# Final stage of a hybrid decoder step: sums of residual and expert rows moved from VectorE to TensorE for four of nine tiles

## The chip, the cores and the metric

The kernel runs on one core of one Trainium2 chip. The metric is the device time of one execution in microseconds (us), lower is better. Engine names in the views: PE is TensorE's matmul, PEld its weight load, DVE is VectorE, ACT is ScalarE, POOL is GpSimd, SP is SyncE; SPq and ACTq are the DMA issues of SP and ACT.

## The reference

One decoder layer over 1048 rows (16 meta tokens, 1024 prompt tokens, 8 sample tokens) of width 1024, fp32. After the mixers (short gated convolution and gated DeltaNet), each row goes through a hierarchical mixture of experts, which picks two of 32 experts per row, and a final RMSNorm:

```python
def _rmsnorm(x, w):
    x32 = x.astype(jnp.float32)
    y = x32 * lax.rsqrt(jnp.mean(x32 * x32, axis=-1, keepdims=True) + EPS) * w.astype(jnp.float32)
    return y.astype(x.dtype)
...
    x = x + jnp.concatenate([y_a, y_b], axis=-1) @ w_out
    x = x + _moe(_rmsnorm(x, norm_ffn), rg_w, rg_b, re_w, re_b, w_gate, w_up, w_down)
...
    y_prompt = _rmsnorm(xp, norm_final)[:, N_META:]
    y_sample = _rmsnorm(xs, norm_final)
```

For the final stage this means: each row of the result is the residual row x plus two expert rows, divided by the root of the mean of its squares, times the weight row `norm_final`.

## The kernel before

The kernel runs in stages: a front stage with the input projection and the mixers, a short stage for the sample tokens, a routing stage with the output projection and the router, the expert stage, and the final stage. The residual rows stay in SBUF as `b.x1`, [128, 9, 1024]. The expert stage takes one expert block of up to 128 rows after the other: GpSimd gathers its rows, TensorE transposes them (`turn`, L1811) and multiplies them (`gate_up`, L1829, and `down`, L1854), ACT and VectorE scale the halves of the product (L1865, L1872), and GpSimd scatters them to a DRAM tensor `b.ye` (L1802) that has two rows for each token, one per chosen expert. 32 blocks run in the main part, and up to 16 overflow blocks behind it, each in a branch (`further`, L1904); in this execution two of them are taken.

The final stage is `final_parts` (L2030). It works on nine tiles of 128 rows, the last of 24 rows. It has no program of its own on the engines: its parts are called at the end of each engine's program of the expert stage.

- SP (`loads`) first waits until all scatters have landed, a chain of branches over the overflow blocks (L1942). Then it issues, for each tile t, the loads of `y0[t]` (L2046) and `y1[t]` (L2047), 512 KB each, without a wait between them, and after tile 0 the load of the weight row `wn` (L2049). Each tile has its own buffers, in SBUF that the expert weights used before.
- VectorE (`scales`) waits for `wn`. For each tile it waits for both loads of the tile, adds `y0` to `x1` (L2086) and `y1` to `x1` (L2088), and then scales the tile before (L2080): row times rstd times `wn`, written over `y1`. So its order is add 0, add 1, scale 0, add 2, scale 1, and so on to add 8, scale 7, scale 8.
- ACT (`norms`) takes for each tile the sum of squares (L2062, with an accumulator read), Ln (L2065) and Exp (L2068), and then issues the store of the tile before (L2057), once it is scaled.
- TensorE has nothing to do in this stage.

Of the kernel before, what the change touches and what calls it, by code (L numbers as in the profile page):

```python
# [9 lines left out]
ALU = mybir.AluOpType  # L10
ACT = mybir.ActivationFunctionType
# [10 lines left out]
TILES = 9  # L22
# [59 lines left out]
def later(i):  # L82

    return not isinstance(i, int) or i > 0
# [1684 lines left out]
def expert_stage(nc, m, s, b, io):  # L1769

    ps = b.psum
# [10 lines left out]
    q = {n: s.pair("e_" + n) for n in names}  # L1782
# [23 lines left out]
    def turn(pe, q, k):  # L1806

        for g in range(2):
            for j in range(4):
                kk = 4 * g + j  # L1810
                ins = nc.tensor.transpose(ps[:, 2 + g, j * P:j * P + C], xg[k][:, kk:kk + KD * (P - 1) + 1:KD],  # L1811
                                          b.ident[0:C, 0:C])
        ins.then_inc(q.turned, 1)
# [9 lines left out]
    def gate_up(pe, q, p, n, k):  # L1823
        pe.wait_ge(q.xt_ok, 2 * n + 2)
        for g in range(2):
            for f in range(KF):
                o = (g * KF + f) * P
                for kk in range(KD):
                    ins = nc.tensor.matmul(ps[:, p, o:o + C], b.slots[k][g][:, kk, f * P:f * P + P],  # L1829
                                           xt[p][:, kk, :], start=(kk == 0), stop=(kk == KD - 1))  # L1830
        ins.then_inc(q.gu_ok, 1)
# [15 lines left out]
    def down(pe, q, p, n, k):  # L1847
        pe.wait_ge(q.he_ok, n + 1)
        if later(n):
            pe.wait_ge(q.outa_ok, n)  # L1850
            pe.wait_ge(q.outb_ok, n)
        for c in range(2):
            for f in range(KF):
                ins = nc.tensor.matmul(ps[0:C, 4 + 2 * p + c, :], he[p][:, f, :],  # L1854
                                       b.slots[k][2][:, f, c * 512:c * 512 + 512], start=(f == 0), stop=(f == KF - 1))
        ins.then_inc(q.down_ok, 1)
# [25 lines left out]
    def staggered(eng, front, mid, back):  # L1882

        front(block_of(0))
        front(block_of(1))
        mid(block_of(0))
        for j in range(4):
            front(block_of(j + 2))
            mid(block_of(j + 1))
            back(block_of(j))  # L1890
        with eng.Fori(1, 7) as i:
            for j in range(4):
                front(block_of(j + 2, i))
                mid(block_of(j + 1, i))
                back(block_of(j, i))
        for e in (30, 31):
            front(block_of(e))
            mid(block_of(e - 1))
            back(block_of(e - 2))
        mid(block_of(31))  # L1900
        back(block_of(30))
        back(block_of(31))

    def further(eng, body):  # L1904

        count = eng.to_reg(eng.value_load(b.ove[0:1, OV:OV + 1], min_val=0, max_val=OV))

        def both(n):
            for p in range(2):
                with eng.If_lt(eng.to_reg(2 * n + p), count):  # L1910
                    body(2 * n + p, p, n)

        both(0)
        with eng.Fori(1, OV // 2) as n:
            both(n)
        return count

    def nothing(x):
        pass

    final = final_parts(nc, m, s, b, io)

    with nc.Block() as block:
        @block.sync
        def _(sp):
            with sp.Fori(0, 7) as i:
                for k in range(4):
                    sp.wait_ge(main[k % 2].down_ok, 2 * i + k // 2 + 1)
                    load_expert(sp, b, io, 4 * i + 4 + k, k)

            def body(v, p, n):
                if later(n):
                    sp.wait_ge(more[p].down_ok, n)
                else:
                    sp.wait_ge(main[p].down_ok, NE // 2 - 1)
                e = sp.value_load(b.ove[0:1, bass.ds(v, 1)], min_val=0, max_val=NE - 1)
                load_expert(sp, b, io, e, p, more_w[p])
            count = further(sp, body)
            for p in range(2):
                sp.wait_ge(main[p].scattered, 16 * (NE // 2))  # L1940
            for v in range(OV):
                with sp.If_lt(sp.to_reg(v), count):  # L1942
                    sp.wait_ge(more[v % 2].scattered, 16 * (v // 2 + 1))
            final.loads(sp)
# [59 lines left out]
        @block.tensor  # L2004
        def _(pe):
            def front(x):
                if later(x.last_n):
                    pe.wait_ge(x.last.xt_ok, 2 * x.last_n)
                pe.wait_ge(gathered[x.k], 16 * (x.r + 1))
                turn(pe, x.q, x.k)  # L2010

            def mid(x):
                pe.wait_ge(b.w_landed[x.k], 48 * (x.r + 1))
                gate_up(pe, x.q, x.p, x.n, x.k)

            staggered(pe, front, mid, lambda x: down(pe, x.q, x.p, x.n, x.k))
            for p in range(2):
                pe.wait_ge(main[p].outa_ok, NE // 2)
                pe.wait_ge(main[p].outb_ok, NE // 2)

            def body(v, p, n):
                pe.wait_ge(more_gathered[p], 16 * (n + 1))
                turn(pe, more[p], p)
                pe.wait_ge(more_w[p], 48 * (n + 1))
                gate_up(pe, more[p], p, n, p)
                down(pe, more[p], p, n, p)
            further(pe, body)


def final_parts(nc, m, s, b, io):  # L2030

    m.at = b.R2
    y0 = [m.place(f"y0_{t}", [P, D]) for t in range(TILES)]
    y1 = [m.place(f"y1_{t}", [P, D]) for t in range(TILES)]
    wn = m.place("wn", [P, D])
    w_in, e_in, add0, x2_ok, sq, ln, rs, o_ok, left = (
        s("wn_in"), s.pair("ye_in", TILES), s("f_add"), s("x2_ok"), s("f_sq"), s("f_ln"), s("f_rs"), s("f_ok"),
        s("y_out"))

    def rows(t):  # L2040
        return P if t < 8 else LAST

    def loads(sp):
        for t in range(TILES):
            n = rows(t)
            sp.dma_start(y0[t][0:n, :], b.ye[t * P:t * P + n, :]).then_inc(e_in[t], 16)  # L2046
            sp.dma_start(y1[t][0:n, :], b.ye[TOK + t * P:TOK + t * P + n, :]).then_inc(e_in[t], 16)  # L2047
            if t == 0:
                sp.dma_start(wn[:, :], io.norm_final.partition_broadcast(P)).then_inc(w_in, 16)  # L2049

    def norms(act):
        nc.scalar.preload_act_table_set("natural_log_exp_and_others")

        def send(t):
            n = rows(t)
            act.wait_ge(o_ok, t + 1)
            act.dma_start(io.y[t * P:t * P + n, :], y1[t][0:n, :]).then_inc(left, 16)  # L2057

        for t in range(TILES):
            n = rows(t)  # L2060
            act.wait_ge(x2_ok, t + 1)
            nc.scalar.activation(y0[t][0:n, :], b.x1[0:n, t, :], ACT.Square, accum_out=b.stat[0:n, t, 0:1]  # L2062
                                 ).then_inc(sq, 1)
            act.wait_ge(sq, t + 1)
            nc.scalar.activation(b.stat[0:n, t, 1:2], b.stat[0:n, t, 0:1], ACT.Ln, scale=1.0 / D,  # L2065
                                 bias=b.eps[0:n, :]).then_inc(ln, 1)
            act.wait_ge(ln, t + 1)
            nc.scalar.activation(b.stat[0:n, t, 2:3], b.stat[0:n, t, 1:2], ACT.Exp, scale=-0.5).then_inc(rs, 1)  # L2068
            if t >= 1:
                send(t - 1)  # L2070
        send(TILES - 1)
        act.wait_ge(left, 16 * TILES)

    def scales(dve):
        dve.wait_ge(w_in, 16)

        def scale(t):
            n = rows(t)
            dve.wait_ge(rs, t + 1)
            nc.vector.scalar_tensor_tensor(y1[t][0:n, :], b.x1[0:n, t, :], b.stat[0:n, t, 2:3], wn[0:n, :],  # L2080
                                           ALU.mult, ALU.mult).then_inc(o_ok, 1)

        for t in range(TILES):
            n = rows(t)
            dve.wait_ge(e_in[t], 32)
            nc.vector.tensor_tensor(b.x1[0:n, t, :], b.x1[0:n, t, :], y0[t][0:n, :], ALU.add).then_inc(add0, 1)  # L2086
            dve.wait_ge(add0, t + 1)
            nc.vector.tensor_tensor(b.x1[0:n, t, :], b.x1[0:n, t, :], y1[t][0:n, :], ALU.add).then_inc(x2_ok, 1)  # L2088
            if t >= 1:
                scale(t - 1)  # L2090
        scale(TILES - 1)

    f = Shared()
    f.loads, f.norms, f.scales = loads, norms, scales
    return f


# [75 lines left out]
```

## Time and profile before

| | us |
|---|---|
| runs shown, median of 3 | 1212.77 |
| lowest and highest | 1210.85, 1213.52 |
| the profiled execution, its own time | 1210.12 |
| its span in the trace | 1208.3 |
| busy: PE / DVE / ACT / POOL | 1026.7 / 450.9 / 371.7 / 158.3 |

The span is the time from the first to the last record of the profiled execution. The granted clock is the share of TensorE's 2.4 GHz that it was given; 0.50 is 1.2 GHz. A DMA share of 1.00 means that the sixteen DMA engines of the core were busy all the time. The two levels to keep apart are the shares over the whole span and what happens in the last 43 us, where the final stage lies (its first load is issued at about 1165 us).

### The profile page before, as it was taken

The page shows a single profiled execution, that of the slowest core. Times are in us where ns is not written, and L with a number is a line of the kernel's source. Part 1 is how long each engine was busy: PE and PEld are TensorE (multiplying, and loading weights), DVE is VectorE, ACT ScalarE, POOL GpSimd, SP SyncE. Part 2 cuts the span into 40 slices and gives each one's busy share as a digit, 9 for nine tenths or more (in the row PEclk, how much of TensorE's full clock was granted, in tenths as well). Part 3 has the DMA queues.
Part 4 walks back from the last instruction along what each step waited for, and adds up shares of the span by engine and source line. Part 5 has one row for each costly group of instructions (what it writes and reads, how often), then busy time and mean ns, then how long its engine had stood idle before and what let it go on. Part 6 is the DMA issues. An engine that isn't in the chain of part 4 may idle for free. (4 is left out here: it accounts for less than half of the span.)

```text
span 1208.3 us, 16435 instructions
## 1 busy us (share of the span) xinstructions
PE 1026.7 (85%) x6572; PEld 917.4 (76%) x6572; DVE 450.9 (37%) x666; ACT 371.7 (31%) x736; POOL 158.3 (13%) x145
## 2 busy tenths in 40 slices
PE   5779999979999999584999914999999999999720
PEld 4669999979999999573777614888888888887510
DVE  5356777892534352334222163111111111111028
ACT  5466776323334343103222100122122121121114
POOL 3011111211101010020000012021121221211000
PEclk9899999999999999766999956999999999999875
DMA  5103666427555541373111174388878878888047
GB/s 205 28 32 109 154 152 165 126 71 225 148 140 146 151 136 24 119 283 122 70 70 70 39 300 175 121 321 316 334 300 307 328 293 321 320 334 314 33 150 298
DMA packets 117658, 221.97 MB, mean 184 GB/s; under 512 B 68316, under 2 KB 81686, under 8 KB 108766
## 3 DMA queue, kind: packets, MB, share of 16 engines
q1 hardware_dynamic: 106618, 199.66, 49.4%
q0 software_dynamic: 9792, 17.19, 3.8%
q10 hardware_dynamic: 1188, 4.29, 0.9%
q8 instruction: 41, 0.67, 0.2%
q14 instruction: 19, 0.16, 0.0%
HBM read 192.33 MB, written 47.26 MB: 198 GB/s over the span
## 5 line engine op out<-in xcount | busy, mean ns | idle before, releaser
L1085 PE MATMUL psum<-hh,wh 128*128 128x350 f32 x672 | 227.8, 339 | 13.1 <-ACT acc L649 8.1
L1085 PE MATMUL psum<-hh,wl 128*128 128x350 f32 x672 | 221.6, 330 | 0.0
L1085 PE MATMUL psum<-hl,wh 128*128 128x350 f32 x672 | 221.1, 329 | 0.0
L1085 PEld LDWEIGHTS psum<-hh,wh 128*128 128x128 f32 x672 | 131.0, 195 | 15.4 <-ACT acc L649 8.6
L1829 PE MATMUL psum<-xgt,wg 128*128 128x128 f32 x1088 | 131.6, 281 | 4.4 <-ACT xgt L1820 4.4
L1829 PEld LDWEIGHTS psum<-xgt,wg 128*128 128x128 f32 x1088 | 128.9, 198 | 5.4 <-issue 5.4
L1085 PEld LDWEIGHTS psum<-hl,wh 128*128 128x128 f32 x672 | 130.9, 195 | 0.9
L1085 PEld LDWEIGHTS psum<-hh,wl 128*128 128x128 f32 x672 | 130.4, 194 | 0.0
L1829 PE MATMUL psum<-xgt,wu 128*128 128x128 f32 x1088 | 127.1, 275 | 0.0
L1854 PE MATMUL psum<-wd,he 128*128 128x512 f32 x272 | 122.4, 593 | 2.8 <-DVE he L1844 2.8
L1829 PEld LDWEIGHTS psum<-xgt,wu 128*128 128x128 f32 x1088 | 124.2, 192 | 0.0
L569 POOL TENSOR_TENSOR wl<-wst,wh 128x1024 fp32r<-128x1024 f32 x28 | 67.9, 2426 | 395.5 <-ACT wh L592 395.5
L1841 DVE SCALAR_TENSOR_TENSOR ge<-thx,psum 128x256 f32<-128x256 f32 x34 | 14.3, 422 | 279.2 <-ACT thx L1835 279.2
L1854 PEld LDWEIGHTS psum<-wd,he 128*128 128x128 f32 x272 | 49.2, 191 | 52.4 <-issue 49.2
L848 DVE SCALAR_TENSOR_TENSOR acc<-raw,cqw,acc 128x1072 f32<-128x1072 f32 x36 | 70.3, 1953 | 26.9 <-ACT acc L631 26.0
L1835 ACT ACTIVATE thx<-psum 128x256 f32<-128x256 f32 x34 | 13.0, 383 | 212.1 <-PE psum L1829 212.1
L1802 POOL DMA_INDIRECT expert_rows<-out,slot_rows x34 | 34.1, 1004 | 335.1 <-DVE out L1872 275.2
L1716 PE MATMUL psum<-wo_hi,yt_hi 128*128 128x512 f32 (+1 forms) x144 | 47.9, 415 | 19.6 <-DVE wo_lo L1562 19.6
L1865 ACT ACTIVATE out<-psum,slot_w 128x512 f32<-128x512 f32 x34 | 23.4, 687 | 110.2 <-PE psum L1854 110.2
L1811 PEld LDWEIGHTS psum<-ident,xg 128*128 128x128 f32 x272 | 36.8, 192 | 25.4 <-issue 17.2
L1872 DVE TENSOR_SCALAR out<-psum,slot_w 128x512 f32<-128x512 f32 x34 | 25.5, 751 | 80.6 <-PE psum L1854 80.6
L1820 ACT ACTIVATE xgt<-psum 128x512 f32<-128x512 f32 x68 | 36.9, 595 | 51.8 <-PE psum L1811 45.8
(322 smaller groups left out, 1342.6 us busy)
## 6 DMA issues: line engine op xcount, KB each, us to landing
wg<-w_gate SPq DMA_DIRECT2D x34, 1024.0 KB, 4.9
wu<-w_up SPq DMA_DIRECT2D x34, 1024.0 KB, 8.0
wd<-w_down SPq DMA_DIRECT2D x34, 1024.0 KB, 11.8
wst<-w_in SPq DMA_DIRECT2D x28, 512.0 KB, 4.2
y<-expert_rows SPq DMA_DIRECT2D x16, 512.0 KB, 11.1
ck<-qkv_rows SPq DMA_DIRECT2D x9, 702.0 KB
qkv_rows<-acc SPq DMA_DIRECT2D x12, 520.0 KB, 6.1
xb<-x SPq DMA_DIRECT2D x8, 512.0 KB, 4.1
```

Source lines behind the costliest of these rows:

```text
L569: nc.gpsimd.tensor_tensor(wl[n % 3][:, :, :], wst[n % 3][:, :, :], wh[n % 2][:, :, :].bitcast(F32), ALU.subtract).then_inc(wl_ok, 1)
L848: stt(ac[:, 0:QLEN], rw[:, q:q + QLEN], w[:, q:q + 1], ac[:, 0:QLEN], ALU.mult, ALU.add).then_inc(taps if q < KQ - 1 else conv_ok, 1)
L1085: ins = mm(ps[:, c, 0:ZC], w[:, kk, :], a[:, kk, c * ZC:(c + 1) * ZC], start=(kk == 0 and q == 0), stop=(kk == KD - 1 and q == 2))
L1716: ins = mm(ps[0:n, 2 * (t % 2) + c, :], y, w[:, c * 512:c * 512 + 512], start=(kk == 0 and q == 0), stop=(kk == KD - 1 and q == 2))
L1802: pool.indirect_dma_start(b.ye, bass.IndirectOffsetOnAxis(ap=b.slot_rows[:, 1, e:e + 1].bitcast(U32), axis=0), out[p][:, :], None, bounds_ ...
L1811: ins = nc.tensor.transpose(ps[:, 2 + g, j * P:j * P + C], xg[k][:, kk:kk + KD * (P - 1) + 1:KD], b.ident[0:C, 0:C])
L1820: nc.scalar.activation(xt[p][:, 4 * g:4 * g + 4, :], bank4(ps, 2 + g, P, C), ACT.Copy).then_inc(q.xt_ok, 1)
L1829: ins = nc.tensor.matmul(ps[:, p, o:o + C], b.slots[k][g][:, kk, f * P:f * P + P], xt[p][:, kk, :], start=(kk == 0), stop=(kk == KD - 1))
L1841: nc.vector.scalar_tensor_tensor(ge[p][:, :, :], th[p][:, :, :], 1.0, g[:, 0:KF], ALU.add, ALU.mult).then_inc(q.ge_ok, 1)
L1854: ins = nc.tensor.matmul(ps[0:C, 4 + 2 * p + c, :], he[p][:, f, :], b.slots[k][2][:, f, c * 512:c * 512 + 512], start=(f == 0), stop=(f == ...
L1865: nc.scalar.activation(out[p][:, 0:512], ps[0:C, 4 + 2 * p, :], ACT.Copy, scale=weight(e)).then_inc(q.outa_ok, 1)
L1872: nc.vector.tensor_scalar(out[p][:, 512:D], ps[0:C, 5 + 2 * p, :], weight(e), None, ALU.mult).then_inc(q.outb_ok, 1)
```

## The change

For tiles 0, 2, 4 and 6 (`SUMMED`) TensorE makes the sum of `x1`, `y0` and `y1` in PSUM: each of the three is multiplied by the identity (`b.ident`) as the stationary operand, in two products of 512 columns, and the six products of a tile accumulate in two banks. The four tiles use two pairs of banks in turn, so tile 4 waits until tile 0 is scaled, and tile 6 until tile 2 is. The products of the residual rows of tiles 0 and 2 are issued before the wait for any load. ACT's square and VectorE's scaling of these tiles read PSUM. VectorE makes no additions for them. The other five tiles stay as they are. The order of the tiles on each engine is not changed.

```diff
             further(pe, body)
+            final.sums(pe)
...
+SUMMED = (0, 2, 4, 6)
...
+    def in_psum(t):
+        return ps[0:rows(t), 2 * bank_of(t):2 * bank_of(t) + 2, :]
...
         for t in range(TILES):
             n = rows(t)
-            act.wait_ge(x2_ok, t + 1)
-            nc.scalar.activation(y0[t][0:n, :], b.x1[0:n, t, :], ACT.Square, accum_out=b.stat[0:n, t, 0:1]
-                                 ).then_inc(sq, 1)
+            if t in SUMMED:
+                act.wait_ge(summed, SUMMED.index(t) + 1)
+                nc.scalar.activation(y0[t][0:n, :].rearrange("p (c n) -> p c n", c=2), in_psum(t), ACT.Square,
+                                     accum_out=b.stat[0:n, t, 0:1]).then_inc(sq, 1)
+            else:
+                act.wait_ge(x2_ok, added.index(t) + 1)
+                nc.scalar.activation(y0[t][0:n, :], b.x1[0:n, t, :], ACT.Square, accum_out=b.stat[0:n, t, 0:1]
+                                     ).then_inc(sq, 1)
...
             dve.wait_ge(rs, t + 1)
+            if t in SUMMED:
+                nc.vector.scalar_tensor_tensor(y1[t][0:n, :].rearrange("p (c n) -> p c n", c=2), in_psum(t),
+                                               b.stat[0:n, t, 2:3], wn[0:n, :].rearrange("p (c n) -> p c n", c=2),
+                                               ALU.mult, ALU.mult).then_inc(o_ok, 1)
...
         for t in range(TILES):
             n = rows(t)
+            if t not in SUMMED:
+                dve.wait_ge(e_in[t], 32)
+                nc.vector.tensor_tensor(b.x1[0:n, t, :], b.x1[0:n, t, :], y0[t][0:n, :], ALU.add).then_inc(add0, 1)
+                dve.wait_ge(add0, added.index(t) + 1)
+                nc.vector.tensor_tensor(b.x1[0:n, t, :], b.x1[0:n, t, :], y1[t][0:n, :], ALU.add).then_inc(x2_ok, 1)
             if t >= 1:
                 scale(t - 1)
         scale(TILES - 1)
 
+    def sums(pe):
+        mm = nc.tensor.matmul
+
+        def add(t, a, first):
+            n = rows(t)
+            for c in range(2):
+                ins = mm(ps[0:n, 2 * bank_of(t) + c, :], b.ident[0:n, 0:n], a[0:n, c * 512:c * 512 + 512],
+                         start=first, stop=(a is y1[t]))
+            return ins
+
+        for i, t in enumerate(SUMMED):
+            if i >= 2:
+                pe.wait_ge(o_ok, SUMMED[i - 2] + 1)
+            add(t, b.x1[:, t, :], True)
+            if i == 1:
+                for q in SUMMED[0:2]:
+                    pe.wait_ge(e_in[q], 32)
+                    add(q, y0[q], False)
+                    add(q, y1[q], False).then_inc(summed, 1)
+            if i >= 2:
+                pe.wait_ge(e_in[t], 32)
+                add(t, y0[t], False)
+                add(t, y1[t], False).then_inc(summed, 1)
```

## Rows read from the trace of the kernel before

**Rows 1.** The page's first line: the span.

```profile
span 1208.3 us, 16435 instructions
```

**Rows 2.** The chain of waits, final stage: start us, us, what.

```profile
1166.80 8.53 DMA y<-expert_rows
...
1175.35 1.24 DVE x L2086
...
1196.99 1.15 DVE x L2086
...
1204.72 1.27 DVE y L2080
```

**Rows 3.** The timeline, final stage: start us, us, engine, line, operation, shapes [idle before].

```profile
1161.90 1.28 ACT L2052 ACT_TABLE_LOAD   x1 [3.94 <-issue]
...
1172.68 1.23 DVE L2086 TENSOR_TENSOR x<-x,y 128x1024 f32<-128x1024 f32 x1 [14.65 <-DMA wn<-norm_final]
...
1177.87 1.06 ACT L2062 ACTIVATE y<-x 128x1024 f32<-128x1024 f32 x1 [0.96 <-DVE x L2088]
...
1179.37 0.20 ACT L2068 ACTIVATE stat<-stat 128x1 f32<-128x1 f32 x1
1179.38 0.40 ACTq L2057 DMA_DIRECT2D y<-y  x1
```

**Rows 4.** Line L2047, loads of y1: all nine, then tile 2's and tile 6's.

```profile
L2047 SPq DMA_DIRECT2D y<-expert_rows x9: 426/591/1812, 1165.4 to 1176.6; - x9
...
DMA to landing us min/median/max: 4.4/11.6/20.3
...
L2047 SPq DMA_DIRECT2D y<-expert_rows x1: 441/441/441, 1167.8 to 1167.8; - x1
...
DMA to landing us min/median/max: 10.1/10.1/10.1
...
L2047 SPq DMA_DIRECT2D y<-expert_rows x1: 706/706/706, 1173.2 to 1173.2; - x1
...
DMA to landing us min/median/max: 17.7/17.7/17.7
```

**Rows 5.** DMA queues from 1179.4 to 1195.3 us: packets, MB, share of 16 engines.

```profile
DMA packets 1780, 6.42 MB, mean 404 GB/s; under 512 B 212, under 2 KB 212, under 8 KB 1780
...
q1 hardware_dynamic: 1166, 4.15, 66.3%
q10 hardware_dynamic: 614, 2.27, 35.8%
```

**Rows 6.** Groups by line and form: busy us, mean ns | idle before.

```profile
L1571 DVE TENSOR_TENSOR x<-psum,xt 128x1024 f32<-128x1024 f32 x8 | 9.7, 1219 | 2.8 <-PE psum L1716 2.8
...
L2080 DVE SCALAR_TENSOR_TENSOR y<-x,stat,wn 128x1024 f32<-128x1024 f32 x8 | 10.2, 1277 | 0.0
...
L2062 ACT ACTIVATE y<-x 128x1024 f32<-128x1024 f32 x8 | 8.5, 1057 | 24.3 <-DVE x L2088 24.3
```

**Rows 7.** TensorE's timeline, last three blocks: start us, us, instructions.

```profile
1122.53 1.97 PE L1811 MATMUL psum<-ident,xg 128*128 128x128 f32 x8 [1.99 <-issue]
1127.65 6.31 PE L1829 MATMUL psum<-xgt,wg 128*128 128x128 f32 x32 [3.16 <-ACT xgt L1820]
1133.80 3.74 PE L1829 MATMUL psum<-xgt,wu 128*128 128x128 f32 x32
...
1153.54 3.70 PE L1854 MATMUL psum<-wd,he 128*128 128x512 f32 x8 [1.38 <-DVE he L1844]
```

**Rows 8.** Two stretches: us, busy (x) of PE, PEld, DVE, ACT, POOL, granted clock, DMA.

```profile
1123.00:1124.00 1.00, 1.00 (x6) 1.00 (x6) 0.00 (x0) 0.00 (x0) 0.13 (x1) 0.50 0.32 127
1133.00:1134.00 1.00, 1.00 (x11) 1.00 (x10) 0.00 (x0) 0.00 (x0) 0.00 (x0) 1.00 0.00 0
```

**Rows 9.** Two stretches of a run of identity products (L1384) from 530.6 us.

```profile
531.70:535.10 3.40, 3.40 (x18) 3.40 (x18) 2.35 (x4) 0.00 (x0) 0.00 (x0) 0.50 1.09 350
535.10:538.50 3.40, 3.40 (x30) 3.40 (x30) 3.20 (x5) 0.00 (x0) 0.00 (x0) 0.93 0.41 83
```

More of the change, by code:

```diff
@@ L2038, in final_parts, with bank_of @@
         s("y_out"))
+    ps = b.psum
+    summed = s("f_summed")
+    added = [t for t in range(TILES) if t not in SUMMED]
     def rows(t):
         return P if t < 8 else LAST
+    def bank_of(t):
+        return SUMMED.index(t) % 2
+    def in_psum(t):
+        return ps[0:rows(t), 2 * bank_of(t):2 * bank_of(t) + 2, :]
     def loads(sp):
@@ L2079, in scale @@
             dve.wait_ge(rs, t + 1)
-            nc.vector.scalar_tensor_tensor(y1[t][0:n, :], b.x1[0:n, t, :], b.stat[0:n, t, 2:3], wn[0:n, :],
-                                           ALU.mult, ALU.mult).then_inc(o_ok, 1)
+            if t in SUMMED:
+                nc.vector.scalar_tensor_tensor(y1[t][0:n, :].rearrange("p (c n) -> p c n", c=2), in_psum(t),
+                                               b.stat[0:n, t, 2:3], wn[0:n, :].rearrange("p (c n) -> p c n", c=2),
+                                               ALU.mult, ALU.mult).then_inc(o_ok, 1)
+            else:
+                nc.vector.scalar_tensor_tensor(y1[t][0:n, :], b.x1[0:n, t, :], b.stat[0:n, t, 2:3], wn[0:n, :],
+                                               ALU.mult, ALU.mult).then_inc(o_ok, 1)
         for t in range(TILES):
             n = rows(t)
[L2085 to L2088, printed above, removed]
+            if t not in SUMMED:
[3 more added lines that the diff above has]
+                nc.vector.tensor_tensor(b.x1[0:n, t, :], b.x1[0:n, t, :], y1[t][0:n, :], ALU.add).then_inc(x2_ok, 1)
             if t >= 1:
@@ L2091, in scales @@
         scale(TILES - 1)
+    def sums(pe):
[19 more added lines that the diff above has]
+                add(t, y1[t], False).then_inc(summed, 1)
     f = Shared()
-    f.loads, f.norms, f.scales = loads, norms, scales
+    f.loads, f.norms, f.scales, f.sums = loads, norms, scales, sums
     return f
```

## The prediction

> **What bounds the kernel now.** I read the page first: the span is 1208.3 us [rows 1], and the profiled execution itself took 1210.12 us, so 1.82 us lie around the span. Its time is 2.65 us under the median of the runs shown (1212.77). I therefore work out a difference inside the trace and take it off the median.
>
> Next the chain of waits over the final stage [rows 2]. From 1175.35 us to the end it is VectorE without a break, and what stands before it is a transfer of expert rows that lands at 1166.80 + 8.53 = 1175.33. Read alone, the chain says that VectorE bounds the stage: tile 1 starts at 1175.35 and tile 7 at 1196.99, 3.61 us for each tile, which are two additions and one scaling.
>
> The third view, the transfers [rows 4, 5], qualifies this. SP issues all eighteen loads of expert rows at once, between 1165.0 and 1178 us. The last full load (tile 7, y1) is issued at 1175.0 and takes 20.3 us: it lands at 1195.3, only 1.7 us before VectorE turns to tile 7. Between 1179.4 and 1195.3 the queues move 6.42 MB at 404 GB/s, 4.15 MB of loads on q1 and 2.27 MB of results on q10, and their packets fill 66.3% + 35.8% of the sixteen engines' time. So two limits run almost side by side, VectorE and the DMA engines. What a lighter VectorE can win is the distance between them.
>
> TensorE does nothing in this stage. ACT is not near the limit: square, accumulator read, Ln and Exp of a tile run from 1177.87, and the result of the tile before goes out at 1179.38, in a cycle of 3.61 [rows 3].
>
> **The change part by part.**
>
> *Removed: eight additions on VectorE* (tiles 0, 2, 4, 6). Tile 0's pair ran from 1172.68, while VectorE would otherwise have waited for tile 1 until 1175.33 [rows 2, 3]; taking it off is worth nothing. The other three pairs lie in the unbroken stretch. A pair is 3.61 less a scaling of about 1.2, so 2.4 us, and 3 x 2.4 = 7.2 us is what the change would give if nothing else held VectorE.
>
> *Changed: ACT's square and VectorE's scaling read PSUM.* A 128x1024 VectorE operation that reads PSUM took 1219 ns, and the SBUF scaling 1277; the SBUF square took 1057 [rows 6]. I take the same prices for PSUM. The bounds are -0.05 and +0.3 us each, since I have no row of a 1024-wide square from PSUM. On the path after the last landing there is only one such scaling, tile 6's.
>
> *Added: 24 identity products of 512 columns on TensorE.* Their nearest row is the down projection: four fp32 products of 128x512, shown as eight matmul instructions, take 3.70 us at the full clock [rows 7], so about 0.43 us per instruction and 0.86 us per product. Residual rows are two products (1.7 us), the two expert rows four (3.45 us). At the lower clock everything takes twice as long: the 32 instructions that began at 1127.65 took 6.31 us and the next 32 took 3.74, while the granted clock was 0.50 before (1.2 GHz) and 1.00 after (2.4 GHz) [rows 7, 8]. The first 32 hold both levels; it is the doubling of a tile from 5.2 to 10.3 us that is the upper bound.
>
> *When TensorE can begin.* Its last work starts at 1153.54 and takes 3.70. Then come the branches over overflow blocks that aren't there; ACT, after its last piece, reached its table load at 1161.90 [rows 3], and I take that as the latest start. The residual products of tiles 0 and 2 need no transfer and end between 1162 and 1168.7, before tile 0's rows land at 1165.4 + 4.4 = 1169.8 [rows 4]. They are hidden at either clock.
>
> *The schedule by hand, clock cold at each restart.* Each burst finds TensorE idle for over 1 us before it. In [rows 7], a stop before 1122.53 gave slow transposes, and the burst from 1127.65 became fast at about 1133, after 5 us. I take that 5 us.
> Tile 0's sum: 1169.8 to 1175.6. Its statistics take ACT 1.75 (1177.87 to the Exp's end before 1179.6); VectorE, busy with tile 1 until 1177.8, loses nothing by it.
> Tile 2's rows land at 1167.8 + 10.1 = 1177.9 [rows 4]. Cold for 5 us (6 of 8 instructions), then fast: ready at 1183.7. Its statistics: 1185.5. VectorE, done with tile 3 at about 1183.5, waits 2 us here, and so does tile 3's square, which stands behind tile 2's in ACT's order. Results 1, 2 and 3 leave later by as much, at 1185.5, 1187.2 and 1190.7, where before the cycle of 3.61 from 1179.38 sent them at 1183.0, 1186.6 and 1190.2.
> TensorE then runs without a stop: residual of tile 4 to 1185.4, its expert rows to 1188.9, residual of tile 6 to 1190.6; its bank is free since the scaling of tile 2 ended at 1186.7. Tiles 3 to 5 land between 1177.9 and 1190.9, evenly spaced at about 1181, 1184 and 1188, each before it is asked for. Tile 6's rows land at 1173.2 + 17.7 = 1190.9 [rows 4], so its sum is ready at 1194.3 and its statistics at 1196.1.
> VectorE: scaling 3 ends at 1188.4, additions 5 at 1190.9, scaling 4 at 1192.1, scaling 5 at 1193.9. Then it needs tile 7's rows.
>
> *When tile 7 lands now.* It needs the 4.15 MB of loads that were left at 1179.4, plus the results W that go out in between: 1179.4 + (4.15 + W)/0.404. Before, W was 2.27 MB and this gives 1195.3. Now five results are issued by 1192.7 and the fifth is hardly served: W is about 2.1 to 2.4, so 1194.9 to 1195.6. I take 1195.4. One result more or less moves it by 0.52/0.404 = 1.3 us.
>
> *The sum.* VectorE starts tile 7 at 1195.4 in place of 1196.99: 1.6 us sooner. From there the order is unchanged (additions 7, scaling 6, additions 8, scaling 7, scaling 8), 9.0 us from 1196.99 to 1204.72 + 1.27 [rows 2], and 2.3 us of last write. Scaling 6 needs its statistics by 1197.9; they are there at 1196.1, with 1.8 us to spare. So 1208.3 - 1.6 = 1206.7 for the span, 1208.5 for a profiled execution, and 1212.77 - 1.6 = 1211.2 for the median. The 7.2 us shrink to 1.6 because VectorE ends its work on tile 5 at 1193.9 and then waits for a transfer.
>
> The Trainium skill, "DMA: Bandwidth & Descriptors", gives 435 GB/s as the ceiling of the fabric. The trace has 404 in the full stretch. By the page's figure tile 7 would land at 1194.2, a gain of 2.8 us; I go by the row.
>
> **The rivals.**
>
> *Loads land sooner (faster, 22%).* If late sums hold one more result back, W falls to 1.6 and tile 7 lands at 1193.7. VectorE, by the schedule, gets there at 1193.9: gain 3.1 us, 1209.7. If the sums of tiles 2 and 4 come as early as in the next rival, scaling 5 ends at 1192.6, and the most that any landing can give is 4.4 us, 1208.4. For it: in the schedule results 1 to 3 leave later. Against: they are issued only 2.5 us late at most and catch up by the fifth. It decides from 0.8 us sooner than I forecast.
>
> *TensorE late at tile 6, clock lost before it (no change, 18%).* If the early sums run fast (tile 2 ready at 1181.3, tile 4 at 1186.4), TensorE has done all it can by 1188.1 and idles until 1190.9 or, with more results out, 1192. The clock falls again and the sum takes 6 us: ready at 1197 to 1198, statistics 1199 to 1199.8, scaling 6 then 1 to 2 us late. Gain 0.6 to loss 0.4: about 1212.6.
>
> *Identity products never bring the clock up (slower, 12%).* Then tile 2 is ready at 1184.7, tile 4 (12 instructions of 0.86) at 1195.0 and tile 6 at 1205.2; statistics 1207.0, scaling 6 1208.2, additions 8 1210.6, then 1.75 + 1.27: the last scaling ends at 1213.6 instead of 1205.99, 7.6 us later, 1220.4. It decides once tile 6's sum comes after 1200.1. Against it: a run of 128-column products with the identity as moving operand started at 530.6; its clock was 0.50 until 535 and 0.93 in the slice after [rows 9].
> The Trainium skill, "TensorE: Matmul & The Clock Gate", section "Part 4: PE-mode transpose", says that the full clock doesn't engage for transposes, which are products with the identity too. These sums are ordinary products, and rows 9 show such a run rising.
>
> *PSUM reads at the dear end, or TensorE held up by its instruction supply (slower, 6%).* Several tenths on each step and a late start would bring scaling 6 to about 1202, where before it began 2.4 us behind 1196.99, at 1199.4: loss 2.6, 1215.4.
>
> *The forecast: VectorE waits for tile 7 (42%), gain 0.4 to 2.4 us*, 1210.4 to 1212.4.
>
> **How the numbers follow.** About 0.2% (2.4 us) is what a measurement of this kernel can tell from no change. The forecast lies inside it, but near its edge, and the three runs shown span 2.7 us. So of its 42% I give 6 to faster; with the early landing that makes 28% less 2 that may read as no change: 26% faster. No change: 36 + 18 + 2 and 1 of the last rival, 57%. Slower: 12 + 5 = 17%. The range goes from the most that an early landing can give (1208.4) to scaling 6 at 1202 (1215.4) and leaves out the case of a clock that stays down. The likeliest case alone has 1210.4 to 1212.4.
>
> **What would show it right or wrong.** Right: in the trace after, VectorE's additions of tile 7 are preceded by idle time that ends with a transfer of expert rows, at about 1195; VectorE shows further idle time of about 2 us before scaling 2, released by ACT's statistics, and that by TensorE; DMA share still near 1 from 1170 to 1195. Matmul starts 0.43 us apart in tile 4 show the full clock, 0.86 the lower one. Wrong: VectorE busy without a gap to the end; the wait before scaling 6 on ACT and TensorE; or tile 7's landing more than 1 us off.

## The result, and the profile after

The changed kernel took 1206.92 us, median of 5 runs (1202.76 to 1207.93), against 1213.52 us for the kernel before (5 runs; one of them, at 2179.81, is left out of the ratio). The ratio is 0.9946, with a 95% interval of 0.9923 to 0.9969: 6.6 us faster by the medians (6.2 if that run is left out of the median too). The forecast was 1211.2, with 1208.4 to 1215.4 as the range, and no change as the likeliest outcome (57%). The time lies under the range.

The profiled execution took 1206.96 us, with this span:

```profile
span 1205.2 us, 16523 instructions
```

So between the two profiled executions the span shrank by 3.1 us, not by 6.6. The chain of waits of the changed kernel (start us, us, what) now runs through a transfer where it ran through VectorE [rows 2]:

```profile
1174.33 19.41 DMA y<-expert_rows
1193.76 1.24 DVE x L2111
...
1201.58 1.27 DVE y L2104
```

Its last full load is issued at 1174.33 and lands 19.4 us later, and VectorE starts tile 7 on it. I measure everything below from the issue of the first load of expert rows (1164.99 us before, 1164.57 after), so that the stages ahead drop out. Tile 7's additions then start at 31.9 us before and at 29.2 after, and the stage up to the span's end takes 43.3 and 40.6 us: 2.7 us less. The other 0.4 us of the spans lie ahead of the stage.

The timeline of the changed kernel, in the same columns as [rows 3, 7]:

```profile
1163.96 6.71 PE L2124 MATMUL psum<-x,ident 128*128 128x512 f32 x8 [7.15 <-issue]
1170.51 3.60 PE L2124 MATMUL psum<-y,ident 128*128 128x512 f32 x8
1174.26 1.22 DVE L2111 TENSOR_TENSOR x<-x,y 128x1024 f32<-128x1024 f32 x1 [16.65 <-DMA y<-expert_rows]
...
1176.78 5.40 PE L2124 MATMUL psum<-y,ident 128*128 128x512 f32 x8 [2.68 <-DMA y<-expert_rows]
1182.01 1.88 PE L2124 MATMUL psum<-x,ident 128*128 128x512 f32 x4
1182.21 1.02 ACT L2077 ACTIVATE y<-psum 128x1024 f32<-128x1024 f32 x1 [3.73 <-PE psum L2124]
...
1183.73 3.60 PE L2124 MATMUL psum<-y,ident 128*128 128x512 f32 x8
1183.92 1.28 DVE L2100 SCALAR_TENSOR_TENSOR y<-psum,stat,wn 128x1024 f32<-128x1024 f32 x1 [1.73 <-ACT stat L2087]
...
1188.88 3.67 PE L2124 MATMUL psum<-y,ident 128*128 128x512 f32 x8
...
1193.76 1.22 DVE L2111 TENSOR_TENSOR x<-x,y 128x1024 f32<-128x1024 f32 x1 [1.20 <-DMA y<-expert_rows]
```

To be seen there: a full-clock sum takes 3.60 us for the eight instructions of the two expert rows, and the residual products at the lower clock 6.71. VectorE idles 1.73 us ahead of scaling 2, for ACT's statistics, which stood behind TensorE (3.73 us of idle on ACT). And it idles 1.20 us ahead of tile 7, for its load. A scaling from PSUM takes 1.28 us, as from SBUF, and a square 1.02, where one from SBUF takes 1.06 [rows 6].

The same kernel by stretches (us, busy of PE, PEld, DVE, ACT, POOL, granted clock, DMA share, GB/s):

```profile
1164.00:1170.00 6.00, 6.00 (x7) 2.48 (x8) 0.00 (x0) 0.00 (x0) 0.00 (x0) 0.50 0.72 237
1170.00:1174.00 4.00, 4.00 (x10) 1.52 (x8) 0.00 (x0) 0.00 (x0) 0.00 (x0) 0.99 0.99 377
...
1177.00:1182.00 5.00, 5.00 (x8) 1.99 (x8) 4.38 (x4) 1.42 (x4) 0.00 (x0) 0.67 1.02 402
1182.00:1192.00 10.00, 10.00 (x25) 4.29 (x23) 7.04 (x7) 6.52 (x16) 0.00 (x0) 1.00 1.03 419
```

TensorE began at 1.2 GHz, was at 2.4 GHz from 1170 on, lost the clock again in the 2.7 us in which it waited for tile 2, and had it back within 5 us of work; from 1182 to 1192 it worked without a stop at the full clock. The DMA queues between 1179.0 us and tile 7's landing (packets, MB, share of the engines), beside [rows 5]:

```profile
DMA packets 1674, 6.05 MB, mean 409 GB/s; under 512 B 196, under 2 KB 196, under 8 KB 1674
...
q1 hardware_dynamic: 1142, 4.07, 69.0%
q10 hardware_dynamic: 532, 1.98, 33.6%
```

### The profile page after: what moved, and what is told of

Its sections match the earlier page's. It is cut to its first block and busy times, and to the rows that moved or that the text cites. A ratio compares the mean times of both kernels' runs of the same rounds, so it can differ in the third digit from the quotient of the medians.

```text
span 1205.2 us, 16523 instructions
## 1 busy us (share of the span) xinstructions
PE 1053.4 (87%) x6620; PEld 928.3 (77%) x6620; DVE 441.5 (37%) x658; ACT 371.6 (31%) x736; POOL 158.3 (13%) x145
## 5 line engine op out<-in xcount | busy, mean ns | idle before, releaser
L1716 PE MATMUL psum<-wo_hi,yt_hi 128*128 128x512 f32 (+1 forms) x144 | 47.8, 415 | 19.5 <-DVE wo_lo L1562 19.5
L1820 ACT ACTIVATE xgt<-psum 128x512 f32<-128x512 f32 x68 | 36.9, 595 | 51.7 <-PE psum L1811 45.8
```

What stands on the lines that cost most here:

```text
L1716: ins = mm(ps[0:n, 2 * (t % 2) + c, :], y, w[:, c * 512:c * 512 + 512], start=(kk == 0 and q == 0), stop=(kk == KD - 1 and q == 2))
L1820: nc.scalar.activation(xt[p][:, 4 * g:4 * g + 4, :], bank4(ps, 2 + g, P, C), ACT.Copy).then_inc(q.xt_ok, 1)
```

## The experiments

Each kernel below was run 12 times beside 35 runs of the kernel before, on one of three chips (the first measurement stands apart: 5 runs of each). "Stage" is the time from the first load's issue to the span's end in the kernel's profile; "tile 1" and "tile 7" are the starts of their additions on VectorE from the same issue.

| kernel | ratio (95% interval) | stage | tile 1 | tile 7 |
|---|---|---|---|---|
| before, first profile | | 43.3 | 10.4 | 31.9 |
| before again | 1.0005 (0.9990 to 1.0020) | 43.5 | 10.5 | 32.0 |
| changed, first measurement | 0.9946 (0.9923 to 0.9969) | 40.6 | 9.7 | 29.2 |
| changed again | 0.9984 (0.9971 to 0.9998) | 40.6 | 9.7 | 29.2 |
| changed, third | 0.9984 (0.9972 to 0.9997) | 40.6 | 9.5 | 29.1 |
| changed, fourth | 0.9993 (0.9977 to 1.0009) | 40.7 | 9.7 | 29.3 |
| no sums | 1.0014 (1.0000 to 1.0029) | 43.7 | 11.0 | 32.2 |
| late stores | 1.0024 (1.0010 to 1.0037) | 44.3 | 9.5 | 27.4 |
| one tile | 1.0000 (0.9988 to 1.0012) | 41.8 | 10.2 | 30.4 |
| five tiles | 1.0003 (0.9987 to 1.0019) | 42.5 | 10.3 | 30.0 |
| five tiles, SP stores held | 0.9983 (0.9970 to 0.9996) | 39.0 | 9.4 | 27.3 |
| before, SP stores held | 1.0006 (0.9990 to 1.0023) | 42.5 | 9.5 | 31.0 |
| changed, SP stores held | 0.9982 (0.9961 to 1.0004) | 39.3 | 10.1 | 27.8 |
| no sums, SP stores held | 0.9979 (0.9961 to 0.9997) | 39.2 | 9.5 | 26.6 |

The column for tile 1 is a warning. Its rows land before any result leaves (the first store is issued 13.5 us after the first load or later), and still they are taken up between 9.4 and 11.0 us. The two runs with "no sums", which issue the same loads and differ only in their stores, have 11.0 and 9.5. So a difference of under 1 us between two of these stages, each profiled once, can lie in how soon the first loads came.

**The kernel before, again.** No edit.

> The kernel before, unchanged, timed against itself and profiled once more. Theory A (the gain of the change lies in the final stage alone, and what was over the forecast is in which execution was profiled): ratio 1.000 within 0.2%; in the profile, the first load of expert rows to the start of VectorE's additions of tile 7 takes 31.9 us as in the first profile, or up to 1 us more, and the span is 1208 to 1212. Theory B (the time of the whole program shifts by 0.2% or more from one loading of a program to the next, so that some 3 us of the measured difference are no effect of the change): the ratio's interval does not hold 1, or the stages ahead of the final stage differ by over 2 us from the first profile.

The ratio is 1.0005 and the stage 43.5 us: the stage repeats to 0.2 us, and what theory A named holds. Theory B's second clause holds too: this span is 1211.9 us, 3.6 longer than the first profile's, and its stage begins 3.45 us later (1168.44 against 1164.99). The output projection (L1716), 470 us ahead of the change, shows where most of it arose. The first row is the first profile's of the kernel before, the second this one's; the two times are the first and last start:

```profile
L1716 PE MATMUL psum<-wo_hi,yt_hi x144: 388/396/763, 560.0 to 690.8; 128*128 128x512 f32 x128, 128*24 128x512 f32 x16
```

```profile
L1716 PE MATMUL psum<-wo_hi,yt_hi x144: 387/396/767, 561.4 to 694.6; 128*128 128x512 f32 x128, 128*24 128x512 f32 x16
```

130.8 us against 133.2 for the same products, with a granted clock over 560 to 700 us of 0.94 against 0.93. That is 2.4 of the 3.45 us. Over the fourteen profiles of this study the stage begins between 1163.10 and 1168.44 us, and the start follows that clock: in eight profiles TensorE was busy for 129.6 to 129.8 us of that stretch (clock 0.94) and the stage begins at 1164.3 to 1165.3, in five for 131.9 to 132.2 us (0.93) and it begins at 1166.8 to 1168.4, in one for 128.7 us (0.95) and it begins at 1163.1. The kernel before is in the first group once and in the second once, so one program can fall in either. Of the nine profiles of kernels with sums on TensorE eight begin at 1165.3 or sooner, of the five others one; fourteen profiles don't tell whether that is chance. On this chip 35 runs of the kernel before went from 1204.67 to 1214.06 us. That is a spread over three times the effect of the final stage.

**The changed kernel, again.** No edit.

> The changed kernel, unchanged. Theory A: ratio 0.994 to 0.998, tile 7's additions start 29 to 30 us after the first load's issue, with VectorE idle before them for a transfer. Theory B: the ratio moves away from 0.9946 by over 0.3% while the final stage takes as long as in the first profile of it.

Ratio 0.9984, stage 40.6 us, VectorE idle 1.30 us ahead of tile 7. In the trace theory A's numbers hold, but its ratio of 0.994 to 0.998 doesn't: 0.9984 lies just over it. Theory B holds (the ratio moved by 0.38% while the stage stayed). So the stage's effect repeats, and the total's doesn't.

**No sums.** The kernel before, with this edit, which leaves the expert rows of four tiles out of the result:

```diff
-            act.wait_ge(x2_ok, t + 1)
+            if t in SUMMED:
+                act.wait_ge(e_in[t], 32)
+            else:
+                act.wait_ge(x2_ok, added.index(t) + 1)
...
-            dve.wait_ge(e_in[t], 32)
-            ... the two additions ...
+            if t not in SUMMED:
+                dve.wait_ge(e_in[t], 32)
+                ... the two additions ...
```

> The kernel before without the eight additions of tiles 0, 2, 4 and 6 (their expert rows are left out of the result) and without any TensorE work: ACT squares the residual rows as soon as the tile's loads have landed. This is the change with TensorE's sums free and at once. Landing-bound theory: the same time as the changed kernel within 1 us, with VectorE idle before tile 7's additions; results leave up to 3 us sooner, so tile 7 lands up to 1.3 us later. Rival (the sums of TensorE are late and cost time): 2 us or more faster than the changed kernel, additions of tile 7 start 2 us sooner.

I expected the changed kernel's time, with tile 7 up to 1.3 us later. It came 3.0 us later, and the stage was as long as before the change. VectorE does five tiles' additions and nothing on TensorE is waited for, and yet:

```profile
1194.06 0.34 ACTq L2062 DMA_DIRECT2D y<-y  x1
1194.29 1.28 DVE L2088 SCALAR_TENSOR_TENSOR y<-x,stat,wn 128x1024 f32<-128x1024 f32 x1 [0.58 <-ACT stat L2076]
...
1196.49 0.34 ACTq L2062 DMA_DIRECT2D y<-y  x1
1199.45 1.23 DVE L2095 TENSOR_TENSOR x<-x,y 128x1024 f32<-128x1024 f32 x1 [3.87 <-DMA y<-expert_rows]
```

VectorE sits idle for 3.87 us ahead of tile 7. The fifth result is issued 26.8 us after the first load, a sixth at 29.3, and from 1181.6 to 1199.4 us the queues carried this:

```profile
q1 hardware_dynamic: 1215, 4.34, 63.3%
q10 hardware_dynamic: 748, 2.76, 38.9%
```

2.76 MB of results went out while the last loads were awaited, 0.78 MB more than in the changed kernel; at 0.4 MB/us that is 1.9 of the 3.0 us. The remaining microsecond is in 0.27 MB more of loads left (0.7 us) and in a lower rate, 399 GB/s in place of 409. Those 0.7 us aren't the stores' doing: in this profile the loads were behind before the first store was issued. The other 2.3 us are nearly the changed kernel's whole 2.7: stores that leave too soon can take back almost all that VectorE's removed additions give. The Trainium skill, "DMA: Bandwidth & Descriptors", section "Queues, rings and completion order", says that an SDMA engine takes turns between the queue rows that have work for it, a packet at a time. The shares above agree: a queue of stores takes its part of the rate although only the loads are waited for.

**Late stores.** The changed kernel, with this edit in ACT's loop:

```diff
-            if t >= 1:
+            if t == TILES - 3:
+                act.wait_ge(e_in[t + 1], 32)
+                for q in range(t):
+                    send(q)
+            if t >= TILES - 2:
                 send(t - 1)
```

> The changed kernel, but no result leaves until tile 7's rows have landed: ACT then issues the stores of tiles 0 to 5 in a row. If loads and stores share the rate (landing-bound theory), tile 7 lands 1.98 MB / 0.409 = 4.8 us sooner, near 24.4 us after the first load's issue, and VectorE then starts tile 7 only when it is done with tile 5, some 1.5 to 2.5 us sooner than in the changed kernel. The six stores then take 7.7 us, and with three more behind them the end is 0 to 2.5 us sooner than the changed kernel's. If the landing is set by something else than the rate shared with the stores, it stays at 29.2 us and the end is later by 1 to 3 us.

The first half holds: tile 7's y1 is issued 9.7 us after the first load and takes 15.4 us in place of 19.4, so it lands at 25.1 us, and VectorE begins it at 27.4 without idle time. This is direct evidence that the stores set the landing. The end was missed: 3.7 us later than the changed kernel's. The cause is in ACT's own queue, which I had priced at 0.34 us per issue:

```profile
1194.06 7.43 ACTq L2071 DMA_DIRECT2D y<-y  x6
...
1201.54 1.06 ACT L2081 ACTIVATE y<-x 128x1024 f32<-128x1024 f32 x1 [7.64 <-issue]
...
1203.28 1.28 DVE L2108 SCALAR_TENSOR_TENSOR y<-x,stat,wn 128x1024 f32<-128x1024 f32 x1 [5.35 <-ACT stat L2087]
```

Six issues in a row took 7.43 us, 1.24 in the mean. They aren't alike: the first took 2.35 us, the next two 0.44 and 0.79, and the last three 1.20 to 1.23. ACT stood in them, so tile 7's square began at 1201.54, 7.2 us after its rows were added, and VectorE idled 5.35 us. VectorE's start on tile 7, without idle time:

```profile
1191.89 1.22 DVE L2115 TENSOR_TENSOR x<-x,y 128x1024 f32<-128x1024 f32 x1
```

**The changed kernel, a third time.** No edit.

> The changed kernel once more, beside the other three. From the first load's issue to the span's end 40.6 us as in both profiles of it (43.3 and 43.5 in both of the kernel before), which is 2.8 us or 0.23%: ratio near 0.9977. If the first measurement's 0.9946 were the effect of the change, the ratio is under 0.996.

0.9984 and 40.6 us, on another chip. The interval holds the 0.9977 of the stage alone, and it rules out a ratio under 0.996: the first measurement's 0.9946 is not the size of the effect.

**One tile.** The changed kernel with `SUMMED = (4,)`, and in `sums` the branch for the first two tiles taken out.

> The changed kernel, but TensorE sums tile 4 alone; eight tiles are added on VectorE. VectorE's work before tile 7 shrinks by one pair, 2.4 us. Landing-bound theory: the stores leave as early as in the kernel before, so tile 7 lands as it did there, 30.3 us after the first load's issue, VectorE has 0.7 us of idle before it, and the stage takes 1.6 us less than before, 41.8 us; three of the changed kernel's four tiles are then worth only 1.2 us together, and that through stores which leave later. Rival (each tile's pair counts alike): 0.7 us less than before, no idle before tile 7, 42.7 us.

The stage is 41.8 us as the landing-bound theory said, but not for its reason: tile 7 landed at 29.4 us, not at 30.3, and VectorE came to it only at 30.4. Its rows show no wait for a load:

```profile
1185.91 1.28 DVE L2104 SCALAR_TENSOR_TENSOR y<-x,stat,wn 128x1024 f32<-128x1024 f32 x1 [0.58 <-ACT stat L2087]
...
1189.89 1.28 DVE L2100 SCALAR_TENSOR_TENSOR y<-psum,stat,wn 128x1024 f32<-128x1024 f32 x1 [0.30 <-ACT stat L2087]
...
1194.68 1.22 DVE L2111 TENSOR_TENSOR x<-x,y 128x1024 f32<-128x1024 f32 x1
```

Of the pair's 2.4 us, 0.9 go to two waits for ACT's statistics (0.58 and 0.30), which before were hidden behind the pair. In this profile one tile brings 1.5 of the changed kernel's 2.7 us. The ratio of 1.0000 shows none of it, and its interval reaches down to 0.9988, just what 1.5 us would be.

**Five tiles.** `SUMMED = (0, 2, 4, 6, 8)`.

> The changed kernel with tile 8 summed on TensorE too. Nothing changes before tile 7 lands (29.2 us after the first load's issue). Behind it, VectorE no longer adds tile 8: additions 7, scaling 6, scaling 7, scaling 8, with tile 8's statistics 1.75 us behind tile 7's: 7.2 us in place of 9.0. Stage 38.8 us, ratio 0.9962. Rival (the end is set by the stores still to be written): the last scaling comes sooner, but the span's end moves by less than 1 us.

Both theories missed: the stage is 1.8 us longer than the changed kernel's. Tile 7 already starts 0.8 us later, at 30.0, though the edit changes nothing ahead of it; the first loads came later in this profile (10.3 us at tile 1). Behind that, VectorE saves tile 8's additions and then waits for tile 8's statistics:

```profile
1193.29 1.89 PE L2124 MATMUL psum<-x,ident 24*24 24x512 f32 x4
1196.06 5.72 PE L2124 MATMUL psum<-y,ident 24*24 24x512 f32 x8 [0.88 <-DMA y<-expert_rows]
```

```profile
1203.52 1.27 DVE L2100 SCALAR_TENSOR_TENSOR y<-psum,stat,wn 24x1024 f32<-24x1024 f32 x1 [3.35 <-ACT stat L2087]
```

The last tile's eight instructions for its expert rows (four products) took 5.72 us in place of 3.6, which is 2.1 of the 3.35 us: the granted clock was 0.93 from 1194 to 1198 us and 0.50 from 1198 to 1202, though TensorE was busy from 1196.06 on. The tile that I moved stands right ahead of the end, where nothing covers TensorE's slow clock.

**Five tiles, SP stores held.** As above, and in `loads`, with ACT's `send` taken out:

```diff
+        sp.wait_ge(e_in[7], 32)
+        for t in range(TILES):
+            n = rows(t)
+            sp.wait_ge(o_ok, t + 1)
+            sp.dma_start(io.y[t * P:t * P + n, :], y1[t][0:n, :]).then_inc(left, 16)
+        sp.wait_ge(left, 16 * TILES)
```

> As five_tiles, and SP issues all stores, none before tile 7's loads have landed, so that ACT issues nothing and isn't blocked by its queue as in the run with late stores. Landing-bound theory: tile 7 lands 25.2 us after the first load's issue (as with late stores), VectorE is ready for it at 27.4 and doesn't wait for it; from there 7.2 us and the last write of 2.3 us: stage 36.9 us, ratio 0.9947. Rival: six stores issued at 25.2 us take 7.7 us and the next ones queue behind them; SP's issues are slow while the queue is full, and the end is set by the stores, at 38.5 us or later.

This changes three things at once: when the stores leave, the queue that they use (SP's, behind the loads), and ACT, which issues none. VectorE begins tile 7 at 27.3 us without idle time, as expected. The stage is 39.0 us where 36.9 were expected. That lies in the rival's range (38.5 or later), but its mechanism, the stores, accounts for 0.8 of the 2.1 us: 3.1 us pass from the last scaling's end to the span's end where 2.3 were assumed. The rest is ahead of scaling 8, which waits 1.74 us for its statistics:

```profile
1201.34 1.27 DVE L2097 SCALAR_TENSOR_TENSOR y<-psum,stat,wn 24x1024 f32<-24x1024 f32 x1 [1.74 <-ACT stat L2088]
```

Tile 7's load took 16.7 us from its issue, not the 15.4 of the run with late stores, and in the three other runs with SP's stores it took 16.6 to 16.9, with about as many bytes of loads left (4.07 to 4.13 MB, and 4.08 there); why stays open.

**The kernel before, SP stores held.** The same SP and ACT edit on the kernel before.

> The kernel before, with no change to the sums, but SP issues all stores, and none before tile 7's loads have landed. If VectorE bounded the kernel before (theory), tile 7 lands about 25 us after the first load's issue in place of 30.3, VectorE still begins it at 31.9, and the stage keeps its 43.3 to 43.5 us; ratio 1.000. If the landing bounded it, additions of tile 7 start sooner and the stage is shorter by 1 us or more.

Tile 7's load landed after 16.6 us in place of 20.3, and the ratio is 1.0006. The stage is 0.9 to 1.0 us shorter, which by my own bound would speak for the landing. The start decides: here tile 1's rows had come sooner, and VectorE took them up at 9.5 us instead of 10.4 or 10.5:

```profile
1177.04 1.23 DVE L2083 TENSOR_TENSOR x<-x,y 128x1024 f32<-128x1024 f32 x1 [0.20 <-DMA y<-expert_rows]
```

From there to the end it is 33.0 us in this kernel and 33.0 in both profiles of the kernel before. Behind tile 1, VectorE alone bounded it.

**The changed kernel, SP stores held.** The same edit on the changed kernel.

> The changed kernel (tiles 0, 2, 4, 6), with the same SP stores held until tile 7 has landed. Theory: the two belong together: VectorE begins tile 7 at 27.4 us without waiting for a load, 9.0 us of its work and 2.3 us of last write follow: stage 38.7 us, 1.9 us less than the changed kernel's 40.6, ratio 0.996. Rival (the stores pile up behind the landing and set the end): 39.5 us or more.

39.3 us, 1.3 less than the changed kernel in place of 1.9, under the rival's 39.5. Tile 1 started 0.4 to 0.6 us later here than in the changed kernel's profiles, which is most of what is missing. VectorE doesn't wait for tile 7:

```profile
1184.89 1.28 DVE L2097 SCALAR_TENSOR_TENSOR y<-psum,stat,wn 128x1024 f32<-128x1024 f32 x1 [1.53 <-ACT stat L2088]
...
1193.14 1.22 DVE L2108 TENSOR_TENSOR x<-x,y 128x1024 f32<-128x1024 f32 x1
...
1200.95 1.27 DVE L2101 SCALAR_TENSOR_TENSOR y<-x,stat,wn 24x1024 f32<-24x1024 f32 x1 [0.58 <-ACT stat L2088]
```

Its ratio of 0.9982 can't be told from the changed kernel's 0.9993 on the same chip.

**No sums, SP stores held.** The same edit on the run without sums.

> The run without sums (tiles 0, 2, 4 and 6 leave out their expert rows, TensorE idle), with SP stores held until tile 7 has landed. Without it the early stores brought tile 7's additions to 32.2 us. Theory (the stores alone did that): now they start at 25 to 26.5 us, ahead of the 27.4 of the version with sums, and the difference is what TensorE's lateness at tile 2 and ACT's order behind it cost. Rival (something else of that run delayed the loads): the additions of tile 7 stay after 29 us.

The additions of tile 7 start at 26.6 us, in place of 32.2 with the stores let go:

```profile
1193.82 1.23 DVE L2092 TENSOR_TENSOR x<-x,y 128x1024 f32<-128x1024 f32 x1 [0.61 <-DMA y<-expert_rows]
```

The stores did most of that, not all: in the first 14.4 us, ahead of any store, the loads had moved 5.04 MB here and 4.75 there, some 0.7 us at 0.4 MB/us. Against the version with TensorE's sums tile 7 starts 1.2 us sooner, but the stage is only 0.1 us shorter, since 3.5 us pass behind the last scaling in place of 2.4.

**The changed kernel, a fourth time.** No edit.

> The changed kernel for a fourth time, for the size of its effect on the whole time. Two measurements gave 0.9984, the first one 0.9946; the final stage alone says 0.9977. If the first was the spread of the stages ahead of the change, this one is between 0.997 and 0.999 and the final stage again 40.6 us.

0.9993, just over the 0.997 to 0.999 that I had expected, with an interval that holds both 0.9977 and 1; stage 40.7 us, with 1.34 us of idle ahead of tile 7.

## Why the prediction was right or wrong

*What bounds the kernel before: right.* VectorE bounded it, with the load of tile 7 close behind. Holding the stores back brought the load 3.7 us forward and left the 33.0 us of VectorE's chain as they were.

*The mechanism: right.* The forecast said that VectorE would wait for tile 7's rows and, for some 2 us, ahead of scaling 2. It waits 1.2 to 1.3 us and 1.6 to 1.7 us in all four profiles. Of the 7.2 us of additions taken off its busy stretch, 2.7 are gained.

*The step that failed inside the stage: the term "when tile 7 lands now".* I took 4.15 MB of loads left, 2.1 to 2.4 MB of results and 404 GB/s, and got 1195.4 us, 30.4 after the first load. Measured were 4.07 MB, 1.98 MB and 409 GB/s, and 29.2 us. Of the 1.2 us, 0.8 lie in the results, and 0.2 each in the loads and the rate. By the prediction's own sign (a landing more than 1 us off) that is a miss, and the stage's gain of 2.7 us lies outside the 0.4 to 2.4 of the forecast case. What I had missed in the results is a gap. The first result was issued sooner than before (13.7 us after the first load in place of 14.4) and the second, behind tile 2's late sum, later (19.1 in place of 18.0). Between 20 and 22 us the results' queue then moved nothing (0.00 MB) while the loads moved 0.84; in the kernel before it moved 0.26 there, and the loads 0.57. My schedule had the second result later still, at 20.5, but I counted the results issued (five, as forecast) and not the time for which their queue stood empty.

*How much of the 2.7 us is the change's.* In the kernel before with SP's stores held, VectorE's chain is the same 33.0 us, but tile 1 came at 9.5 us, as in the changed kernel's profiles (9.5 to 9.7), and its stage is 42.5 us. Against that the changed kernel is 1.8 us shorter, close to the 1.6 of the forecast. Whether the earlier tile 1 comes with the change or by chance isn't shown.

*The step that failed in the sum for the whole time: all that lies ahead of the stage was put at nothing.* I took the stage's gain off the median of three runs. With the stage's own 2.7 us that sum would have given 1210.1, inside the range; so the landing term alone doesn't put the time under it. The other 3.9 of the measured 6.6 us lie outside the stage. What the profiles show there is a spread of 5.3 us from one execution to the next, in groups that go with the clock that the output projection was granted. The medians agree with this: for the kernel before it was 1213.52 in the first measurement and 1209.8 to 1210.3 in three later ones of 35 runs each, for the changed kernel 1206.92 and then 1208.1 to 1208.3. So most of the surplus lies in the runs of the kernel before. That chance put more of them among the late starts is argued, not shown: the runs of the first measurement have no stage times of their own, and its chip isn't on record. Whether something ties the spread to the program that was measured stays open: the profiles lean that way (eight of nine early starts against one of five), the three later comparisons don't, since their medians differ by 1.5 to 2.2 us, less than the stage's own 2.7. I had put the noise of a measurement at 0.2%, from three runs that span 2.7 us; 35 runs span 9.4.

*The ratio: agreement without proof.* The forecast of 1211.2 against 1212.77 is a ratio of 0.9987. Three further comparisons of the same two kernels gave 0.9984, 0.9984 and 0.9993, in the mean 0.9987 too. The stage's 2.7 us are 0.9978 of the whole, and all three intervals hold that as well, so they don't tell the one from the other; that the mean meets the forecast is luck as much as insight. The first measurement doesn't agree with either: both lie outside its interval.

*TensorE's start: a bound that was wrong at no cost.* I took 1161.9 us as the latest start, by ACT's way through the same branches. It began at 1163.96, 7.15 us after its last product, at the lower clock, and tile 0's sum had to wait for the residual products until 1170.5. By then the clock was up, so the sum ran fast and was ready at 1174.1, sooner than the 1175.6 forecast.

*The clock at each restart: right.* Tile 2's sum ran mostly cold and was ready at 1182.2 (forecast 1183.7); from there to tile 6 TensorE never lost the clock. The rival in which identity products leave the clock down is refuted by the four profiles. The rival of a clock lost before tile 6 didn't occur, since TensorE was still on tile 6's residual rows until shortly before its load came; it did occur in the five-tile version, at tile 8.

*PSUM reads: right.* 1.28 us for the scaling, 1.02 for the square, inside the bounds.

*The rival "loads land sooner": in the stage it is what happened, at a smaller size.* It was to decide from 0.8 us sooner than forecast, and the landing came 1.2 us sooner; it had put the results at 1.6 MB, and they were 1.98. Its mechanism, late sums that hold results back, is the gap in the results' queue above, and the run without sums bears it out: with no lateness at all the stage took 43.7 us, no gain, or a gain of some 0.4 us if the 0.7 of late loads are taken off. So the sums' lateness was no cost; it kept the stores out of the loads' way.

## What to carry to other kernels

When an engine that bounds a stage has a transfer close behind it, price the transfer anew for the changed schedule: loads left, stores served meanwhile, and the rate; an engine made faster also stores sooner, and the run without sums lost nearly its whole gain to that. If stores are held back, issue them from an engine that has nothing else to do: on ACT the held stores made the stage 3.7 us longer, on SP 1.3 us shorter. And where an effect of 2 to 3 us is at stake in a kernel of 1200 us, measure it inside the stage, from an event at the stage's start, and look whether that start itself was alike. Here 12 runs against 35 gave the total within 0.13 to 0.16%, and one such comparison of the changed kernel in three could not tell it from no change.

## What the runs showed of the hardware that was not expected

- Six stores of 512 KB issued back to back held ACT for 7.43 us (late stores; the last three 1.20 to 1.23 each), against 0.34 us for one issued alone. On SP the issues grew alike: 0.37, 0.42, 0.79 and then four of 1.19 to 1.20 us (changed, SP stores held).
- The clock of a sum went with what TensorE had done just before: eight 512-column instructions took 3.60 us at the full clock and 6.7 at the lower one (rows of the first timeline above). In the five-tile version it fell to 0.50 during a burst of products with 24 rows, after 0.88 us of idle, while in the version with held stores the same eight took 3.59 us directly behind others. Whether the gap or the 24 rows made the difference isn't shown.
- TensorE needed 7.14 to 7.72 us, in the changed kernel's four profiles, from its last product through branches that aren't taken to its next one; ACT needed 3.94 us for its own way to its next instruction.
